# A hybrid decoder trunk on one core: the depthwise convolution of all four channel groups on VectorE, its running sum and the tie marks in PSUM, three buffers for the q, k and v tiles

## What is computed

```python
h = x + 0.5 * g1 * swiglu(modulate(x, g_ffn1, s1, sc1), w1_gate, w1_up, w1_down)
n = modulate(h, g_mix, s2, sc2)
z = n @ w_in       # conv GLU (2*512) | q | k | v (8x64 each) | indexer q, k, weights | gates (2*1024)
u = a_lin * sigmoid(a_gate)                          # 512 channels
conv_out = silu(layernorm(depthwise_conv31(u) + b_dw)) @ w_conv_out
I[t, s] = sum_h w[t, h] * relu(q_idx[t, h] . k_idx[s])      # keep the 256 largest per prompt token
att = softmax_attention(q, k, v over the kept keys) @ w_attn_o
h = h + g2 * ((sigmoid(g_c) * conv_out + sigmoid(g_a) * att) @ w_out)
h = h + 0.5 * g3 * swiglu(modulate(h, g_ffn2, s3, sc3), w2_gate, w2_up, w2_down)
y = rmsnorm(h)
```

## Time and profile before

| | |
|---|---|
| runs | 2780.43, 2782.2 and 2788.05 us |
| profiled execution | 2788.55 us, span 2786.5 us |
| PE busy | 2562.2 us, 92% of the span |
| DVE busy | 1363.0 us, 49% |
| POOL busy | 957.0 us, 34% |
| ACT busy | 606.3 us, 22% |
| chain that ended last | PE 79%, POOL 6%, DVE 4%, issue 3%, ACT 3%, DMA 2% |

### The profile page before, as it was taken

How to read it: one execution, slowest core, us unless ns; L and a number is a source line. 1 busy time by engine, 2 the same in 40 slices (tenths; PEclk the granted TensorE clock), 3 DMA queues, 4 the chain that set the end, 5 groups by cost and what they waited for, 6 DMA issues and landing times.

```text
span 2786.5 us, 41897 instructions
## 1 busy us (share of the span) xinstructions
PE 2562.2 (92%) x15990; PEld 2377.7 (85%) x15990; DVE 1363.0 (49%) x2413; ACT 606.3 (22%) x1086; POOL 957.0 (34%) x494
## 2 busy tenths in 40 slices
PE   6999999999998788899994687999899999999998
PEld 3899999999997756799994345789799999999998
DVE  3333333333336646799999835453433333333333
ACT  2311010101103233213333346510411000010003
POOL 1232233332233224637999101024033333333333
PEclk7999999999999989999997789999999999999999
DMA  8322222222222412321223500144011111111111
GB/s 272 108 75 75 76 75 75 69 74 75 75 72 91 120 42 57 98 77 52 80 84 132 195 5 1 54 132 134 12 46 46 45 45 45 45 45 45 45 53 63
DMA packets 207603, 209.81 MB, mean 75 GB/s; under 512 B 13087, under 2 KB 160659, under 8 KB 206601
## 3 DMA queue, kind: packets, MB, share of 16 engines
q1 hardware_dynamic: 197324, 181.57, 20.8%
q10 hardware_dynamic: 10181, 26.90, 3.0%
HBM read 172.90 MB, written 28.94 MB: 72 GB/s over the span
## 4 chain that ended last, share of the span: by engine, by line
PE 79%; POOL 6%; DVE 4%; issue 3%; ACT 3%; DMA 2%; SPq 2%; ACTq 1%; DVEq 0%; POOLq 0%
PE main L248 24%; PE main L249 23%; PE main L250 23%; POOL conv_y L1365 4%; SPq L1453 1%; PE main L1654 1%; PE main L1671 1%; PE aux L979 1%; PE aux L1682 1%; POOL wlo L237 1%; DVE pick L1279 1%; PE aux L336 1%; PE main L336 1%; DMA q_d<-zraw 1%; PE aux L394 1%
## 5 line engine op out<-in xcount | busy, mean ns | idle before, releaser
L248 PE MATMUL main<-nhi,whi 128*128 128x352 f32 x3192 | 1042.9, 327 | 22.3 <-DVE nlo L464 17.4
L249 PE MATMUL main<-nlo,whi 128*128 128x352 f32 x3192 | 1029.2, 322 | 0.0
L250 PE MATMUL main<-nhi,wlo 128*128 128x352 f32 x3192 | 1028.2, 322 | 0.0
L235 POOL CAST whi<-raw 128x1024 fp32r<-128x1024 f32 x185 | 201.3, 1088 | 1538.3 <-PE main L250 1207.0
L248 PEld LDWEIGHTS main<-nhi,whi 128*128 128x128 f32 x3192 | 602.6, 189 | 57.2 <-issue 43.5
L249 PEld LDWEIGHTS main<-nlo,whi 128*128 128x128 f32 x3192 | 603.8, 189 | 0.5
L250 PEld LDWEIGHTS main<-nhi,wlo 128*128 128x128 f32 x3192 | 602.0, 189 | 0.5
L237 POOL TENSOR_TENSOR wlo<-raw,whi 128x1024 fp32r<-128x1024 f32 x185 | 466.3, 2521 | 14.8
L686 DVE TENSOR_TENSOR tmp<-main,tmp 128x352 f32<-128x352 f32 x132 | 69.3, 525 | 779.4 <-PE main L250 776.3
L705 DVE SCALAR_TENSOR_TENSOR h<-main,ada,h 128x352 f32<-128x352 f32 (+1 forms) x528 | 296.9, 569 | 114.8 <-PE main L250 114.7
L248 PE MATMUL main<-hid_hi,whi 128*128 128x352 f32 x1056 | 343.2, 325 | 0.0
(11 more groups left out here) (289 smaller groups left out, 2494.9 us busy)
## 6 DMA issues: line engine op xcount, KB each, us to landing
ada_raw<-in_w_ada SPq DMA_DIRECT2D x18, 2048.0 KB, 8.7
raw<-in_w_gate SPq DMA_DIRECT2D x44, 512.0 KB, 3.8
raw<-in_w_up SPq DMA_DIRECT2D x44, 512.0 KB, 3.8
raw<-in_w_down SPq DMA_DIRECT2D x44, 512.0 KB, 3.7
raw<-in_w_in SPq DMA_DIRECT2D x40, 512.0 KB, 3.8
gate_d<-zraw ACTq DMA_DIRECT2D x16, 528.0 KB, 2.7
gates<-gate_d SPq DMA_DIRECT2D x16, 528.0 KB, 4.7
zsw<-zraw ACTq DMA_DIRECT2D x50, 132.0 KB, 2.4
```

The source lines that it names most:

```text
L235: pool.tensor_copy(hi, raw[:, slot]).then_inc(hi_done, 1)
L248: pe.matmul(bank, w_hi[:, w], hi(c), start=(i == 0), stop=False)
L249: pe.matmul(bank, w_hi[:, w], lo(c), start=False, stop=False)
L250: last = pe.matmul(bank, w_lo[:, w], hi(c), start=False, stop=(i == n - 1))
```

## The change

- `zraw` gets a third buffer `zthird`; q, k and v tiles take the three in turn, with three store semaphores, and tile L waits for the store of tile L - 3.
- `equal` of `keep_largest` lies in `aux` (PSUM). The ranking takes as its second input the scores' tile `x`, which at that place holds zeros and large negative numbers, and waits for one more step.
- The products on ACT and the sums on POOL are gone, with their semaphores. DVE does the four groups one after the other (`conv_group`): a first tap into `aux`, a loop of 29 taps in place in `aux` with one step a turn, a last tap from `aux` to `conv_y`.
- PE waits for the whole convolution (`CV_TOTAL`) ahead of turning v; before, it waited there for the six sign steps. SP and PE no longer wait for POOL's sums.

```diff
+        def zrow(L):
+            return zthird[:, :] if Z_Q <= L < Z_GLU and (L - Z_Q) % 3 == 2 else \
+                zraw[:, (L - Z_Q) % 3 if Z_Q <= L < Z_GLU else L % 2, :]
...
+        zthird = place("zthird", [P, TOK], F32, UB + 21504 + 2048)
...
-        equal = place("equal", [P, SEQ], F32, UB + 38144)
+        equal = aux[:, :, :].rearrange("p a n -> p (a n)")
...
-                for i in PRODUCTS_AT.get(L - 3, []):
-                    conv_add(pool, i)
...
-                for i in PRODUCTS_AT.get(L, [])[t:t + 1]:
-                    if i == 0:
-                        act.wait_ge(glu, 1)
-                    conv_product(act, i)
...
             def store(L, dst):
-                act.dma_start(dst, zraw[:, L % 2, :]).then_inc(z_out[L % 2], 16)
+                act.dma_start(dst, zrow(L)).then_inc(z_out[(L - Z_Q) % 3], 16)
...
-                s = L % 2
-                if L >= Z_Q + 2:
-                    act.wait_ge(z_out[s], 16 * ((L - Z_Q) // 2))
-                evac(act, zraw[:, s, :], L, ACT.Copy, weigh)
+                if L >= Z_Q + 3:
+                    act.wait_ge(z_out[(L - Z_Q) % 3], 16 * ((L - Z_Q) // 3))
+                evac(act, zrow(L), L, ACT.Copy, weigh)
...
-                dve.wait_ge(sel_keep, done + 2)
-                dve.tensor_tensor_scan(rank[:, 0:w], equal[:, 0:w], equal[:, 0:w], over[:, i:i + 1], ALU.add, ALU.max)\
+                dve.wait_ge(sel_keep, done + 3)
+                dve.tensor_tensor_scan(rank[:, 0:w], equal[:, 0:w], x, over[:, i:i + 1], ALU.add, ALU.max)\
                     .then_inc(sel_keep, 1)
...
-            conv_first(dve)
-            conv_taps(dve, 1, CW)
+            for c in range(4):
+                conv_group(dve, c)
...
+        def conv_group(dve, c):
+
+            begun = CV_DEC + CW * c
+            y = aux[:, :, :].rearrange("p a n -> p (a n)")
+            dve.wait_ge(cv, begun)
+            dve.tensor_scalar(y, uext[:, c, 0:SEQ], taps[:, c, 0:1], par[:, ROW_BDW + c:ROW_BDW + c + 1], ALU.mult,
+                              ALU.add).then_inc(cv, 1)
+            with dve.Fori(1, CW - 1) as k:
+                dve.wait_ge(cv, begun + k)
+                dve.scalar_tensor_tensor(y, uext[:, c, bass.ds(k, SEQ)], taps[:, c, bass.ds(k, 1)], y, ALU.mult, ALU.add)\
+                    .then_inc(cv, 1)
+            dve.wait_ge(cv, begun + CW - 1)
+            dve.scalar_tensor_tensor(conv_y[:, c, 0:SEQ], uext[:, c, CW - 1:CW - 1 + SEQ], taps[:, c, CW - 1:CW], y,
+                                     ALU.mult, ALU.add).then_inc(cv, 1)
...
-            sp.wait_ge(cv_sum, CW - 1)
...
-            sp.wait_ge(cv_sum, NPROD)
             sp.dma_start(vraw[:, :, :], v_d).then_inc(v_in, 16)
...
             pe.wait_ge(v_in, 16)
-            pe.wait_ge(sel_keep, NSEL)
+            pe.wait_ge(cv, CV_TOTAL)
             for t in range(9):
                 turn_tokens(t, vraw, t)
```

More of the change, by code:

```diff
@@ L866, in post @@
                     pool.tensor_tensor(zsw[:, s, :], zsw[:, s, :], rot[:, 1, :], ALU.mult).then_inc(rope_b, 1)
-                    pool.tensor_tensor(zraw[:, s, :], zraw[:, s, :], rot[:, 0, :], ALU.mult).then_inc(rope_b, 1)
+                    pool.tensor_tensor(zrow(L), zrow(L), rot[:, 0, :], ALU.mult).then_inc(rope_b, 1)
                     pool.wait_ge(rope_b, 3 * n + 2)
-                    pool.tensor_tensor(zraw[:, s, :], zraw[:, s, :], zsw[:, s, :], ALU.add).then_inc(rope_b, 1)
+                    pool.tensor_tensor(zrow(L), zrow(L), zsw[:, s, :], ALU.add).then_inc(rope_b, 1)
                 elif Z_GLU <= L < Z_GATE and (L - Z_GLU) % 2:
@@ L874, in post @@
                         pool.wait_ge(si_sel, 2)
-                        pool.memset(uext[:, :, 0:HIST], 0.0).then_inc(uzero, 1)
+                        pool.memset(uext[:, :, 0:HIST], 0.0)
                     pool.tensor_tensor(uext[:, c, HIST:], zraw[:, 1, 0:SEQ], zraw[:, 0, 0:SEQ], ALU.mult)\
@@ L1003, in evac, with swap @@
                     then(n)
-                for i in PRODUCTS_AT.get(L, [])[t:t + 1]:
-                    if i == 0:
-                        act.wait_ge(glu, 1)
-                    conv_product(act, i)
-        def swap(act, s, rows):
+        def swap(act, L, rows):
             for r in range(0, rows, 32):
                 o = r + 32 if r % 64 == 0 else r - 32
-                act.dma_start(zsw[r:r + 32, s, :], zraw[o:o + 32, s, :]).then_inc(swap_in[s], 16)
+                act.dma_start(zsw[r:r + 32, L % 2, :], zrow(L)[o:o + 32, :]).then_inc(swap_in[L % 2], 16)
         def m1_act(act):
@@ L1026, in m1_act @@
                 act.wait_ge(z_free, 6 + 3 * L + 3)
-                swap(act, L % 2, 64 if L == 0 else P)
+                swap(act, L, 64 if L == 0 else P)
                 if L == 0:
@@ L1088, in m1_act @@
                     store(L, v_d[:, L - Z_V, :])
-            act.wait_ge(z_out[0], 16 * 6)
-            act.wait_ge(z_out[1], 16 * 6)
+            for s in range(3):
+                act.wait_ge(z_out[s], 16 * 4)
             for c in range(4):
@@ L1099, in m1_act @@
                 s, m = L % 2, L - Z_GATE
-                act.wait_ge(z_out[s], 16 * (6 + m // 2))
+                act.wait_ge(z_out[s], 16 * (4 + m // 2))
                 evac(act, zraw[:, s, :], L, ACT.Sigmoid, weigh)
-                for i in PRODUCTS_AT[L][3:]:
-                    conv_product(act, i)
                 act.wait_ge(z_free, 6 + 3 * L + 3)
@@ L1289, in m1_dve @@
             dve.wait_ge(sel_keep, 7 * NSEL)
-            dve.wait_ge(uzero, 1)
             dve.wait_ge(st_e, 2)
@@ L1308, in m1_dve @@
                 .then_inc(cv, 1)
-            conv_first(dve)
-            conv_taps(dve, 1, CW)
+            for c in range(4):
+                conv_group(dve, c)
         CV_DEC = 4 * 2 + 1
[L1313 to L1352, removed]
-            act.activation(product_of(i), uext[:, c, k:k + SEQ], ACT.Copy, scale=taps[:, c, k:k + 1])\
-                .then_inc(cv_prod, 1)
-        def conv_add(pool, i):
-            c = i // (CW - 1)
-            into = zsw[:, 0, 0:SEQ] if i < IN_ZSW else conv_y[:, c, 0:SEQ]
-            y = zsw[:, 0, 0:SEQ] if i <= IN_ZSW else conv_y[:, c, 0:SEQ]
-            pool.wait_ge(cv_start, c + 1)
-            pool.wait_ge(cv_prod, i + 1)
-            if i:
-                pool.wait_ge(cv_sum, i)
-            pool.tensor_tensor(into, y, product_of(i), ALU.add).then_inc(cv_sum, 1)
+        CV_TOTAL = CV_DEC + 4 * CW
@@ L1470, in m2_sp @@
             sp.wait_ge(acc_done, ZDONE)
-            sp.wait_ge(z_out[0], 16 * 14)
-            sp.wait_ge(z_out[1], 16 * 14)
+            sp.wait_ge(z_out[0], 16 * 12)
+            sp.wait_ge(z_out[1], 16 * 12)
+            sp.wait_ge(z_out[2], 16 * 4)
             sp.dma_start(ka[:, :, :], k_d).then_inc(k_in, 16)
```

7 lines of the change are left out of this document (2 added, 5 removed).

## The result

The changed kernel takes 2810.0 us (median; 2807.29 to 2818.52), against 2781.3 for the kernel before in the same set: ratio 1.0104, 95% interval 1.0075 to 1.0133, so 28.7 us slower. Forecast was 39.1 us slower, 2821.

A forecast was written before the change was run, and what follows sets the result against it. The bound was the attention's first VectorE step, where POOL's sums (through v and pages) and DVE's convolution meet. Convolution end 1590.7 plus 64.2 gave 1654.9 against 1615.8, 39.1 us later: 2821 us on the 2782.2 median, range 2796 to 2840.

The forecast's parts named there:

- two lines meet at the attention: Attention's first VectorE step: POOL's sums, through v and the pages, meet DVE's convolution, which ends 28 us ahead.
- Score stage: PE's waits for ACT's weighted scores shrink with three buffers: 11 us less, between 4 and 20; pieces end at 1142.8.
- the third buffer doesn't help: Rival, score stage: POOL's rotations hold DVE just as long; 11 us later than forecast, 2832; no separate chance given.
- Ties and decoder: On DVE after the search: ties 44.5 us (36 to 55) against 96.0, decoder's convolution 12.0 against 14.2.
- Search: DVE's search for the 256th largest score, ahead of the ties: unchanged at 205.6 us of instructions.
- Taps: DVE's convolution, 124 steps: looped steps 1.30 plus gap 0.21; 185.8 us in all (162 to 199), ending at 1590.7.
- Behind the convolution: From convolution end to attention: v, first address fetch, sixteen page loads, landing and the rest, 64.2 us in all.
- Sum: Attention's start: 1590.7 + 64.2 = 1654.9 against 1615.8, so 39.1 us later; nothing behind it differs.
- A free wait: Rival, taps: waiting between taps costs nothing, pitch stays 1.204; attention 2.6 us later, 2785, no change; chance 0.08.
- the case that the prediction put between the two: Taps with a gap of 0.03 and steps of 1.30: 116 x 1.33, 18 us later, still slower.
- The chained step: Rival, taps: sum in PSUM lets steps stream at 1.075; attention 13.4 us sooner, 2769, needs pitch below 1.18; chance 0.05.
- PSUM at half pace: Rival, taps: steps reading and writing PSUM run at half pace, 1.075 more each, some 133 us, 2954; chance 0.04.

The follow-up runs named there:

- e6: Kernel before with only the tie marks in PSUM (PE's wait ahead of v set to the end of the ties): 2785.2 us, ratio 1.0010 to the kernel before.
- e1: The changed kernel with PE turning v and k through the two banks of main alone, not aux: 2769.9 us, ratio 0.9957 to the kernel before.
- e4: The changed kernel with six logits and the value pages of sequences 4 to 7 moved ahead of v: 2793.7 us, ratio 1.0051 to the kernel before.
- e5: The kernel before with only the third buffer for q, k and v tiles added: 2773.5 us, ratio 0.9973 to the kernel before.
- e11: The changed kernel with two buffers again for the q, k and v tiles: 2828.6 us, ratio 1.0143 to the kernel before.
- e2: The changed kernel with the 29 looped taps of each group written out, with constant waits: 2794.6 us, ratio 1.0044 to the kernel before.
- e9: The changed kernel with page numbers kept in registers from the key loads for the value loads: 2795.9 us, ratio 1.0050 to the kernel before.
- e10: The changed kernel with v/k turned through main, taps written out, group 0 back on ACT and POOL, page numbers kept: 2729.1 us, ratio 0.9791 to the kernel before.
- e7: The changed kernel with v/k turned through main, taps written out, group 0 back on ACT and POOL: 2732.8 us, ratio 0.9850 to the kernel before.

## Why the prediction was right, and where its sizes were off

**What bounds.** Right: two lines meet at the attention, and VectorE had slack. e6 shows the slack (time won on VectorE changes nothing), e1 and e4 show that what the change moves behind the convolution is the cost. One reading on the way there does not hold: it was not GpSimd's last sum that held v in the kernel before. That sum ended at 1525.7, and SP loaded v 15 us later. From the chain that ended last in the kernel before, and from SP's timeline there:

```profile
1519.14 2.67 DMA gate_d<-zraw
1521.87 0.33 SPq L1473
```

```profile
1540.88 0.43 SPq L1479 DMA_DIRECT2D vraw<-v_d  x1
```

SP waits for the store of the last gate tile, then loads k, q and four key pages, then v; the store stands on ACT among products that wait for GpSimd's sums. So GpSimd's sums were on the path, but through that store and SP's row. The forecast counts from the end of the convolution and does not use this step.

**Score stage.** Forecast 11 us, the last piece at 1142.8; measured 1131.6 + 9.4 = 1141.0. The waits came out at 13.8, as forecast near 13, and e5 and e11 hold the buffer's worth at about 10. The rival "the third buffer doesn't help" falls.

**Ties and decoder.** Forecast 44.5 and 12.0, measured 42.8 (1337.2 to 1380.0) and 12.1. The first block took 8.1 us against 8.3 from the prices of single lines. Search: 205.6, unchanged.

**Taps.** Forecast 185.8, measured 180.2 (1392.1 to 1572.35): the largest of the sizes that were off. The gap was 0.18 us where I took 0.21, and the step 1.289 where I took 1.30; the gap of L1978, 0.19, was the right row and should have been taken as it stood. The step with its sum in PSUM is 16 ns above the 1.273 from SBUF. The estimate of 0.065 from the Trainium skill (VectorE: DVE Perf Modes, on the TRN2 errata) is four times that; L705's 15 ns came close, in part by luck: its shape is smaller, its output lies in SBUF, and with the pace per column not rounded, (1347 - 673) / 640, it is 18.

**Behind the convolution.** Forecast 64.2, measured 62.4: v and the first fetch 8.6 (9.1 forecast), loads 41.9 (41.05), landing 2.3, from there to the attention 9.6 (11.7). As forecast, logits, k and softmax fit beside the loads, with 12.0 us to spare.

**Sum.** Four misses go the same way, 1.8 + 1.7 + 5.6 + 1.8 us, and with 0.1 the other way from the decoder they turn the 39.1 into the 28.4. The mechanism stood, and almost every term was taken a little dear, the taps most.

**Rivals.** A free wait needs constants, which the change does not have in its loops; e2 has them and takes 15 us less than the change, still 0.4% more than the kernel before: not this rival's pitch of 1.204, but the case that the prediction put between the two. The chained step does not stream: pitch 1.47, and 1.32 in e2, both above 1.18. PSUM at half pace does not occur.

## What to carry to other kernels

Before a running sum goes into a buffer that others use, look who waits for that buffer and what is queued behind the waiting instruction; here two other banks were free for the turn, and using them turned a loss of 1.0% into a gain of 0.4%. A chain of dependent steps in a hardware loop paid 0.17 us at every step here, where written-out steps paid 0.035. A row of loads with numbers fetched one by one is a serial line of its own: a number that is needed twice is fetched once and kept.

## What had not been expected

The fetch of a page's number from DRAM sets the pace of these loads, not the 256 KB behind it. On SP in the change, the loads into registers for the sixteen value pages (ns min/median/max, first and last start):

```profile
L1408 SPq TENSOR_LOAD <-in_page_table_ptr x16: 1018/1258/1582, 1579.0 to 1620.3; - x16
L1408 SPq TENSOR_LOAD <-in_page_table x16: 457/462/639, 1580.1 to 1621.6; - x16
```

For each page a pointer is loaded anew, 1.26 us, and then the number, 0.46; the pointer is the dearer of the two. With both and the register work a page takes 2.6 us, without them some 0.6 (e9 and e10, waits for PE taken off). The prediction had put 2.2 us of a page down to the fetch, but carried the 41 us over as a whole and did not ask whether the numbers could be kept.

The start of an execution is not the same from one to the next: with granted clocks of 0.76 to 0.90 in the first 70 us, and the same code, the first conditioning matmuls into `aux` start at 135.3 us in e9 and at 145.0 in e1. Two traces have to be laid together at a place behind that before differences of 10 us are read from them.

Open is why SP's first fetch behind the loads of k and q, or of v, takes 6 to 8 us where the others take about 2 (in e7 the key pages start at 1474.48 and 1494.50, behind loads issued at 1467.88 and 1486.39). The pointer and the number themselves take long there, 3.15 and 2.39 us, then 4.00 and 1.15; whether the large loads under way at that time are the reason was not tried. Open, too, is which part of the 0.17 us is the register wait, which the register addresses and which the semaphore.
